# A layer norm moved to tokens on partitions, and sliding attention of decoded tokens in column groups

## What is computed

```
def post_norm(x, h, g, b):                    # behind the experts, h is their output
    return layer_norm(ALPHA * x + h, g, b)    # (z - mean) / sqrt(var + eps) * g + b, over D = 1024

def swa_with_buffer(q, kk, vv, sink):         # 8 decoded tokens, each with its own window of 128 keys
    s = einsum('bqhgd,bkhd->bhgqk', q, kk) * C_SCALE      # 2 key heads, 8 query heads to each, 64 wide
    p = sink_softmax(s, mask, sink[None, :, :, None, None])
    return einsum('bhgqk,bkhd->bqhgd', p, vv)
```

## Time and profile before

| | us |
|---|---|
| median of 3 runs | 2436.62 |
| the profiled execution, its own time | 2443.1 |
| its span, first to last instruction | 2440.9 |
| TensorE busy in it | 2295.1 (94%) |
| VectorE, ScalarE, GpSimd busy | 1692.5, 1317.6, 1043.5 |
| mean granted TensorE clock, share of full speed | 0.978 |

### The profile page before, as it was taken

The page is one execution under the profiler, slowest core; times in us unless marked ns, Lnnn a source line. Parts: engine busy times, 40 slices in busy tenths (PEclk is TensorE's granted clock), DMA queues, the critical chain, the costliest instruction groups (busy, mean ns, idle before and its releaser), DMA issues. The chain is left out here.

```text
span 2440.9 us, 46395 instructions
## 1 busy us (share of the span) xinstructions
PE 2295.1 (94%) x15682; PEld 2067.8 (85%) x15682; DVE 1692.5 (69%) x3470; ACT 1317.6 (54%) x2979; POOL 1043.5 (43%) x801
## 2 busy tenths in 40 slices
PE   7797989999999999999979898999999999999997
PEld 7676879999999977888868886999999997788885
DVE  4667558996988655666655464899698884566665
ACT  4214446446776645555546453644577674555554
POOL 4642434997777730000023144389877774000000
PEclk9998999999999999999989899999999999999998
DMA  6424834444444465555535474544444446655552
GB/s 219 146 94 86 355 139 149 155 162 157 141 145 139 145 224 194 187 189 184 186 102 168 130 279 188 173 147 155 164 140 143 142 139 207 200 188 189 184 186 87
DMA packets 115076, 409.31 MB, mean 168 GB/s; under 512 B 19977, under 2 KB 22193, under 8 KB 109489
## 3 DMA queue, kind: packets, MB, share of 16 engines
q1 hardware_dynamic: 110896, 391.45, 47.6%
q0 software_dynamic: 4032, 15.86, 2.0%
HBM read 397.11 MB, written 10.14 MB: 167 GB/s over the span
## 5 line engine op out<-in xcount | busy, mean ns | idle before, releaser
L2075 POOL TENSOR_TENSOR slab_ring_lo<-slab_ring,u_hi 128x512 fp32r<-128x512 f32 x512 | 713.0, 1412 | 199.7 <-ACT u_hi L2169 199.0
L2117 PE MATMUL banks<-operand_hi,u_hi 128*128 128x264 f32 x2048 | 594.6, 290 | 18.5 <-POOL slab_ring_lo L2075 18.3
L2119 PE MATMUL banks<-operand_hi,slab_ring_lo 128*128 128x264 f32 x2048 | 583.1, 285 | 0.0
L2118 PE MATMUL banks<-operand_lo,u_hi 128*128 128x264 f32 x2048 | 581.9, 284 | 0.0
L309 POOL TENSOR_TENSOR slab_ring_lo<-slab_ring,slab_hi 128x512 fp32r<-128x512 f32 x130 | 172.0, 1324 | 647.1 <-ACT slab_hi L299 647.1
L2499 DVE TENSOR_TENSOR operand_lo<-slab_ring,operand_hi 128x512 fp32r<-128x512 f32 x512 | 354.2, 692 | 109.1 <-ACT operand_hi L2471 101.0
L2531 PE MATMUL banks<-operand_hi,w_hi 128*128 128x512 f32 x1024 | 408.9, 399 | 11.9 <-DVE w_lo L2495 11.9
L2169 ACT ACTIVATE u_hi<-slab_ring 128x512 fp32r<-128x512 f32 x512 | 321.8, 630 | 158.6 <-PE banks L2119 158.6
L2532 PE MATMUL banks<-operand_hi,w_lo 128*128 128x512 f32 x1024 | 407.4, 398 | 0.0
L2533 PE MATMUL banks<-operand_lo,w_hi 128*128 128x512 f32 x1024 | 407.3, 398 | 0.0
L2117 PEld LDWEIGHTS banks<-operand_hi,u_hi 128*128 128x128 f32 x2048 | 386.6, 189 | 23.1 <-POOL slab_ring_lo L2075 18.7
(11 more groups left out here) (379 smaller groups left out, 4080.2 us busy)
## 6 DMA issues: line engine op xcount, KB each, us to landing
slab_ring<-in_u SPq DMA_DIRECT2D x256, 512.0 KB
slab_ring<-in_v SPq DMA_DIRECT2D x256, 512.0 KB
slab_ring<-in_proj SPq DMA_DIRECT2D x144, 512.0 KB
cache_k_T<-in_cache_k SPq DMA_DIRECT2D x16, 1024.0 KB, 8.9
cache_v<-in_cache_v SPq DMA_DIRECT2D x16, 1024.0 KB, 13.1
memory_T<-in_mem POOLq DMA_DIRECT2D x2, 1024.0 KB, 7.7
sample_state<-in_state POOLq DMA_DIRECT2D x1, 2048.0 KB, 9.1
out_mem_k_out<-mem_k_T SPq DMA_DIRECT2D x16, 128.0 KB, 2.0
```

What stands on the lines that cost most here:

```text
L2075: nc.gpsimd.tensor_tensor(step.ring_lo[:, s, g * HC:(g + 1) * HC, :], step.slab(s)[:, g * HC:(g + 1) * HC, :], hi[:, buf].bitcast(F32), AL ...
L2117: nc.tensor.matmul(bank, hi[:, buf, k, :], xh[:, c, :], start=(c == 0), stop=False)
L2118: nc.tensor.matmul(bank, hi[:, buf, k, :], xl[:, c, :], start=False, stop=False)
L2119: last = nc.tensor.matmul(bank, step.ring_lo[:, s, c, :], xh[:, c, :], start=False, stop=(c == DC - 1))
```

## The change

It has three parts. (1) The norm behind the experts works with tokens on partitions: during the first 32 slabs of the down product TensorE turns x (six rounds of four transposes, into bank 5), ScalarE copies each round to `z`, and the decoded tokens' residual and norm are done there too; the block behind has 4 residual passes over the banks, `bn_stats` and `bn_aggr` for mean and variance, a root and a reciprocal of one value a token, a normalising pass, and 16 transposes of 128 tokens and 8 of the decoded ones back, from which ScalarE and VectorE write x with scale and shift. (2) y is stored in four DMAs from that block, no longer in one behind it. (3) The decoded sliding attention takes 32 columns of queries (then of probabilities) as weights, mostly zero, and the window's 128 keys (values) as data, in four column groups; one transposing step goes, one at the end comes, and GpSimd makes the zeroed operands and the new key's column in the block ahead. A line of "..." stands for what is left out, and of the last part only the new lines are shown.

```diff
@@ store_result
-                self.store(sp, io["y"], self.x[:])
@@ emit_norm: removed
-def emit_norm(step, block, tag, sub, res, base_bank, residual_steps, tensor_steps, next_slab, early=None, partial=None):
...
@@ window_mixer: buffers and GpSimd of the block window_prompt
+        PAIRS = TS * KV
+        own_q = sb("sample_own_queries1", [P, PAIRS, 32])
+        own_p = sb("sample_own_probabilities", [P, PAIRS, 32])
+        s_own = step.sem("sample_own_operands_ready")
+        s_k = step.sem("sample_key_column_ready")
...
+                step.link(pool, "gpsimd", nc.gpsimd.memset(own_q[:], 0.0))
+                nc.gpsimd.memset(own_p[:], 0.0).then_inc(s_own, 1)
+                pool.wait_ge(s_own, 1)
+                for e in range(2):
+                    rows = slice(e * HD, (e + 1) * HD)
+                    for kv in range(KV):
+                        own = bass.AP(own_q, 40 * kv + 4 * e, [own_q[:].ap[0], [128, TS // 2], [80, 2], [1, 4]])
+                        nc.gpsimd.tensor_copy(own[rows], step.q[rows, 4 * kv:4 * kv + 4, TP:T].rearrange(
+                            "p j (a b) -> p a b j", b=2)).then_inc(s_own, 1)
+                        pool.wait_ge(s_own, 2 + 2 * e + kv)
+                nc.gpsimd.tensor_copy(kx[:, :, :, P - 1], kT[:, :, TP:T].rearrange("p k b -> p b k")).then_inc(s_k, 1)
+                pool.wait_ge(s_k, 1)
...
@@ window_mixer: block window_sample
+                def each_pair(left, right, bank):
+                    for w in range(4):
+                        for q in range(4):
+                            b, kv = 2 * q + w // 2, w % 2
+                            last = nc.tensor.matmul(ps[32 * q:32 * q + 32, bank, 0:P], left[:, b * KV + kv, :], right[:, b, kv, :],
+                                                    start=(w == 0), stop=(w == 3))
+                    return last
                 pe.wait_ge(windows_ready, 32)
                 pe.wait_ge(s_k, 1)
-                for b in range(TS):
-                    for kv in range(KV):
-                        for e in range(2):
-                            rows = slice(e * HD, (e + 1) * HD)
-                            col = (b * KV + kv) * 4
-                            last = nc.tensor.matmul(ps[:, 4 * e, col:col + 4], kx[rows, b, kv, :],
-                                                    step.q[rows, kv * 4:kv * 4 + 4, TP + b], start=True, stop=True)
-                last.then_inc(s_s, 1)
-                pe.wait_ge(s_sc, 1)
-                nc.tensor.transpose(ps[:, 1, 0:P], st[:], step.ident).then_inc(s_t, 1)
+                pe.wait_ge(s_own, 5)
+                each_pair(own_q, kx, 0).then_inc(s_s, 1)
                 pe.wait_ge(s_p, 1)
                 nc.tensor.transpose(ps[:, 2, 0:P], ss[:], step.ident).then_inc(s_pt, 1)
                 pe.wait_ge(s_pc, 1)
                 pe.wait_ge(s_vrow, 16)
-                for b in range(TS):
-                    for kv in range(KV):
-                        col = (b * KV + kv) * 8
-                        last = nc.tensor.matmul(ps[:, 3, col:col + 8], vx[:, b, kv, :], sp_t[:, col:col + 8],
-                                                start=True, stop=True)
-                last.then_inc(s_o, 1)
+                each_pair(own_p, vx, 3).then_inc(s_o, 1)
+                pe.wait_ge(s_or, 1)
+                nc.tensor.transpose(ps[:, 4, 0:P], rows_o[:], step.ident).then_inc(s_oT, 1)
...
-                nc.scalar.activation(ss[:], ss[:], ACT.Exp, bias=sm[:, 0:1], accum_out=sm[:, 1:2])
+                nc.scalar.activation(ss[:], ps[:, 0, 0:P], ACT.Exp, bias=sm[:, 0:1], accum_out=sm[:, 1:2])
                 nc.scalar.activation(sm[:, 2:3], sm[:, 0:1], ACT.Exp, bias=snk[:, HEADS_C:]).then_inc(s_e, 1)
                 act.wait_ge(s_pt, 1)
-                nc.scalar.activation(sp_t[:], ps[:, 2, 0:P], ACT.Copy).then_inc(s_pc, 1)
+                act.wait_ge(s_own, 1)
+                own = bass.AP(own_p, 0, [own_p[:].ap[0], [128, TS // 2], [40, 4], [1, 8]])
+                nc.scalar.activation(own, ps[:, 2, 0:P].rearrange("p (a w r) -> p a w r", w=4, r=8), ACT.Copy).then_inc(s_pc, 1)
+                act.wait_ge(s_o, 1)
+                nc.scalar.activation(rows_o[:], ps[:, 3, 0:P], ACT.Copy).then_inc(s_or, 1)
             @block.vector
             def _(dve):
                 link = lambda ins, wait=True: step.link(dve, "vector", ins, wait)
-
-                nc.vector.tensor_copy(kx[:, :, :, P - 1], kT[:, :, TP:T].rearrange("p k b -> p b k")).then_inc(s_k, 1)
-                for e in range(2):
-                    last = nc.vector.tensor_copy(st[:].rearrange("p (g e j) -> p g e j", e=2, j=4)[:, :, e],
-                                                 ps[:, 4 * e, 0:HD].rearrange("p (g j) -> p g j", j=4))
-                last.then_inc(s_sc, 1)
-                dve.wait_ge(s_t, 1)
-                link(nc.vector.tensor_copy(ss[:], ps[:, 1, 0:P]))
-                link(nc.vector.tensor_reduce(sm[:, 0:1], ss[:], AX, ALU.max, negate=True))
+                link(nc.vector.tensor_reduce(sm[:, 0:1], ps[:, 0, 0:P], AX, ALU.max, negate=True))
...
+                dve.wait_ge(s_oT, 1)
+                o = ps[:, 4, 0:P].rearrange("p (b k e j) -> p k e j b", b=TS, k=KV, e=2)
...
@@ peer_down
-OWN_AT, VALUES_AT, SUM_FROM, UNROLLED = 10, (12, 18), 22, 28
+OWN_AT, VALUES_AT, SUM_FROM, UNROLLED = 10, (12, 18), 22, 32
-    y_s = room[:, 1832:1832 + DC * TS].rearrange("p (c t) -> p c t", c=DC)
-    y_t = big[:].rearrange("p n t -> p (n t)")[:, 0:2 * D].rearrange("p (t d) -> p t d", t=2)
+    small = lambda t: (room[:, 2048 + 20 * t:2060 + 20 * t], room[:, 2060 + 20 * t:2062 + 20 * t],
+                       room[:, 2062 + 20 * t:2063 + 20 * t])
+    flat = big[:].rearrange("p n t -> p (n t)")
+    z = [flat[:, 0:D], flat[:, D:2 * D], flat[0:TS, 2 * D:3 * D]]
+    FREED = -(-3 * D // T)
+    TOKENS_AT = (13, 16, 19, 21, 23, 25)
...
@@ ACT:
-                if n == UNROLLED - 1:
-                    act.wait_ge(s_ys, 1)
-                    nc.scalar.activation(y_s, ps[:, 4, 0:DC * TS].rearrange("p (c t) -> p c t", c=DC), ACT.Copy).then_inc(s_yc, 1)
+                for r in range(6):
+                    if n == TOKENS_AT[r] + 1:
+                        t, g, a, b = token_round(r)
+                        act.wait_ge(s_xt, r + 1)
+                        act.wait_ge(s_wl, FREED)
+                        nc.scalar.activation(z[t][:, g * HALF:(g + 1) * HALF], ps[0:b - a, 5, :], ACT.Copy).then_inc(s_xc, 1)
+                if n == UNROLLED - 2:
+                    act.wait_ge(s_var, 1)
+                    stats, mv, std = small(2)
+                    nc.scalar.activation(std[0:TS], mv[0:TS, 1:2], ACT.Sqrt, bias=step.eps[0:TS]).then_inc(s_std, 1)
@@ DVE:
+                if n == SUM_FROM + 5:
+                    dve.wait_ge(s_xc, 6)
+                    dve.wait_ge(s_ys, 1)
+                    link = lambda ins: step.link(dve, "vector", ins)
+                    stats, mv, std = (part[0:TS] for part in small(2))
+                    for g in range(2):
+                        half = z[2][:, g * HALF:(g + 1) * HALF]
+                        link(nc.vector.scalar_tensor_tensor(out=half, in0=half, scalar=ALPHA, in1=ps[0:TS, (4, 6)[g], :],
+                                                            op0=ALU.mult, op1=ALU.add))
+                        last = nc.vector.bn_stats(stats[:, 6 * g:6 * g + 6], half)
+                    link(last)
+                    nc.vector.bn_aggr(mv, stats).then_inc(s_var, 1)
+                if n == UNROLLED - 1:
+                    dve.wait_ge(s_std, 1)
+                    link(nc.vector.reciprocal(std, std))
+                    link(nc.vector.tensor_scalar(z[2], z[2], mv[:, 0:1], std, ALU.subtract, ALU.mult))
@@ PE:
-                for c in range(DC):
-                    last = nc.tensor.matmul(ps[:, 4, c * TS:(c + 1) * TS], got[:, 0, c * P:(c + 1) * P], group_of,
+                for g in range(2):
+                    last = nc.tensor.matmul(ps[0:TS, (4, 6)[g], :], group_of, got[:, 0, g * HALF:(g + 1) * HALF],
                                             start=True, stop=True)
                 last.then_inc(s_ys, 1)
+            def token_transposes(r):
+                t, g, a, b = token_round(r)
+                if r:
+                    pe.wait_ge(s_xc, r)
+                for k in range(HC):
+                    last = nc.tensor.transpose(ps[0:b - a, 5, k * P:(k + 1) * P], step.x[:, g * HC + k, a:b], step.ident)
+                last.then_inc(s_xt, 1)
             for n in range(UNROLLED):
                 down(n // SLOTS, n % SLOTS, n == 0, False)
                 if n in VALUES_AT:
                     values(VALUES_AT.index(n))
                 if n == SUM_FROM + 1:
                     add_groups()
+                if n in TOKENS_AT:
+                    token_transposes(TOKENS_AT.index(n))
...
@@ the block peer_norm: emit_norm and its steps replaced by
+TOKEN_TILES = ((0, P), (P, TP), (TP, T))
```

(91 more changed lines are left out.)

157 lines of the change are left out of this document (33 added, 124 removed).

## The result

The changed kernel took 2412.27 us (median of 4 runs, 2409.93 to 2413.25) beside 2436.08 for the kernel before (4 runs, 2434.11 to 2438.7); the ratio is 0.9895, 95% interval 0.9881 to 0.9908, that is 25.6 us less (22 to 29). Timed again in a later batch it was 0.989 (0.9875 to 0.9905), 26.8 us less. Forecast were 2410 and 26.5 us.

A forecast was written before the change was run, and what follows sets the result against it. TensorE, busy 94%, bounds the experts' stages; hand-over chains hold the norms. Gains 11.5 + 13.8 + 8.7, less 7.2 and 0.3, make 26.5 us: 2436.6 − 26.5 = 2410.1, range 2402 to 2421.

The forecast's parts named there:

- Norm, layer 0: Norm block behind layer 0's experts: VectorE's chain shrinks from 26.3 to 14.8 us, gain 11.5 (9.5 to 13.5).
- rival (b): Norms and burst: `bn_stats` is slow, 3.5 us for 512 columns; time near 2439, no change; chance 0.03.
- A pair: Layer 0's norm, writing x and its two parts: 1.5 us for each of four pairs of chunks (bounds 1.1 and 2.1).
- Norm, layer 1: Last norm and stores of y: end at 13.2 us instead of 27.0, gain 13.8 (12 to 15).
- Down product: Both layers' down products: transposes and in-line work cost 3.6 us a layer, 7.2 in both (5 to 12).
- The change of kind: Down product: TensorE pays 0.06 to 0.1 us for each of six changes of kind, besides the transposes.
- The stall at slab 28: Down product: VectorE's 3.1 us of decoded-token work at slab 27 delays slab 28, a stall of 0.5 us.
- Rival (a): Down product's in-line work exceeds ScalarE's 0.4 us slack; 0.9 us lost in each of 12 rounds, time 2421; chance 0.09.
- Rival (c): Down product: transposes let TensorE's clock fall for the next slab, 2.8 us each, 12 times; time 2443.7; chance 0.03.
- Rival (d): Norms gain more (pairs in 1.1, stores landing in 2), with the attention at its best: 2402; chance 0.07.
- Decoded attention: `window_sample`: SyncE ends it late and ScalarE starts the following block at 1394.5 instead of 1403.26; gain 8.7 (6.5 to 9.3).
- GpSimd's placements: `window_prompt`: zeroings and placements take 2.5 to 7 us, up to 5.5 covered; cost 0.3 us (0 to 1.5).

The follow-up runs named there:

- the doubled copies: Changed kernel with each of ScalarE's twelve copies of transposed tokens out of PSUM done twice: 2416.45 us, ratio 0.9903 to the kernel before.
- rounds of eight: Changed kernel with each of the twelve rounds of four transposes issued twice: 2420.8 us, ratio 0.9921 to the kernel before.
- attention alone: Kernel before with only the new decoded sliding attention, GpSimd's placements included: ratio 0.9967, 8.1 us less than before.
- the run with the clock held up: Changed kernel with unread identity products in TensorE's pauses in the norms and decoded attention: 2412.72 us, ratio 0.988 to the kernel before.
- the last kernel: Changed kernel with the burst in four pieces, half the normalising on ScalarE and identity products in the norms' pauses alone: 2409.23 us, ratio 0.9881 to the kernel before.

## Why the prediction was right

**The sum.** Forecast 26.5 us, found 25.6 and 26.8, by stages 26.1. Each stage moved as forecast and by about as much; that the sum is met within 1 us is partly luck, since errors of 0.3 to 0.6 in the terms cancel. One slip is in the bounds: the good ends of the terms add up to 32.8 us, so to 2404 and not 2402.

**Norm, layer 0:** 11.5 forecast, 12.5 and 11.1 measured against two traces of the old one (27.51 and 26.13), the mean 11.8. The two old norms differ because TensorE's clock was at 0.50 for 3.4 us of the first (1239.33 to 1242.74) and at 1.00 in that part of the second; the prediction read its rows in the first. `bn_stats` was taken at one pass, 0.65, and is 0.64, so rival (b) is out. Chunk 0 was forecast for t = 8.15 and came at 8.31: TensorE's transposes began at 7.79 instead of 7.7, since a normalising pass takes 0.54, not 0.47, and the first landed after 0.52 instead of 0.45. A pair was forecast at 1.5 and took 1.04 to 1.11, the lower bound: behind one pause of 0.28 VectorE's three instructions hide the hand-overs altogether. So the operands were ready at 13.75 instead of 14.8. The transposes took 0.22 and more at granted clock 0.50, as forecast. The Trainium skill (TensorE: Matmul & The Clock Gate, Part 4) says that transposes don't count as work of TensorE for its clock in the way that products do. The trace agrees as far as it goes: 16 of them between 1244.27 and 1249.24 left the clock at 0.50. But TensorE also stood 1.03 between them, so this doesn't tell the one cause from the other.

**Norm, layer 1:** 13.8 forecast, 13.4 measured. The stores were issued by 10.8 and landed after 2.4, both as forecast; the end came at 13.7 for 13.2, since the last issue's landing took 2.9, not the median 2.4.

**Down product:** 7.2 forecast, 7.8 measured, 3.90 a layer for 3.6, and this near miss is luck: two terms are wrong and nearly cancel. The change of kind, 0.06 to 0.1 in each of six rounds, does not exist: a round costs 0.43 to 0.44, its four transposes. The stall at slab 28 was forecast at 0.5 and is 1.22. The burst itself was sized rightly (3.1 forecast, 2.92 measured). What failed is where it starts. The prediction's "ends at 941.7, 1.9 us behind the slab's start" was read from slab 23 of the old kernel, where no round precedes. In the changed kernel slab 25 carries a round, ScalarE copies it first (951.09), the high and low parts behind come later, and the burst starts about 2.9 behind the start of slab 26 instead of 1.9. Then 2.9 + 2.9 + 0.6 + 0.4 = 6.8 against 5.6: 1.2. One part of the change had moved the point from which another was measured.

**Rival (a)**, that ScalarE's free time doesn't hold the copy: one copy fits, since a round costs just its transposes, but by the doubled copies only 0.27 us are left. With only that much left, the rival was nearer than its chance of 0.09 says. **Rival (c)**, a clock that falls behind a round, is refuted even for rounds of eight. **Rival (d)** had the pairs right (1.1), but the stores landed after 2.4 to 2.9, not 2, and the down products cost more than forecast, not less.

**Decoded attention:** 8.7 forecast, 8.3 to 9.0 measured, with 7.4 for VectorE's end and 7.7 for SyncE's forecast (1393.8 and 1394.13 less 1386.4) and 7.47 and 7.26 measured. "Ended by SyncE, not VectorE" was wrong, by 0.21 in this trace and by 1.14 in the kernel's second one: SyncE's eight issues vary from trace to trace, 3.78 to 5.23 with the same stores on its queue. SyncE does end the block where its issues are slow (attention alone, by 0.19) and once TensorE is fast (8.56 in the run with the clock held up). **GpSimd's placements:** 0.3 forecast, nothing measured; they took 2.65, the low end of 2.5 to 7, and the earlier trace rows had 2.9 to hide them.

**Root's table load:** the Trainium skill (ScalarE: Activation LUTs, What ACT_TABLE_LOAD costs) adds a drain of 1.38 to a load. The trace disagrees again: the load at 961.71 ends at 962.99, the root starts at 963.00, and no stall follows at slab 31. The prediction had given 7.8 as the down products' cost with that drain; that 7.8 was measured is chance, since it comes from the stall at slab 28.

## What to carry to other kernels

Normalise in the layout in which the reduction lies within a partition, and pay for the turn where the turned data is known early, in pieces, beside the large products: 24 transposes cost 2.66 us there, and the norm lost over 11. Work put in line behind a saturated TensorE must be spread over the slabs and timed from the changed schedule, not from the old one: 2.9 us in one piece cost 1.22, in four pieces nothing that shows. When an experiment isolates a stage, compare landmark to landmark: landmark to norm repeated to 0.03 us here where whole runs differed by 4. And look at the stages behind those that were changed: the last kernel won 4.6 us in its own stages and lost 2.4 in one whose code nobody had touched.
